# A gather-fed expert layer on one core: three of every four rows of the second table go to TensorE, one stays with VectorE

## The chip, the cores and the metric

The kernel runs on one core of a Trainium2 chip. The metric is the device time of one execution in microseconds (us); less is better. A core has TensorE (PE: matrix products, with its weight loads listed apart as PEld), VectorE (DVE), ScalarE (ACT), GpSimd (POOL) and SyncE (SP), each working through an instruction stream of its own in order and waiting for the others by semaphores, and sixteen DMA engines that they share.

## The reference

Two layers of a transformer-like block run over five blocks of 128 tokens (one of context, four latent). A layer is a mixer (four attention-like groups and an output product) followed by an expert layer. The mixer is unchanged here; the expert layer, cut to what matters, is this (`p` holds the layer's weights, `xb` is a block of 128 tokens by 1024):

```python
q = (xb @ p['peer_w_q']).reshape(128, 8, 2, 128)
s = jnp.einsum('thpd,pnd->thpn', q, p['peer_sub_keys'])
sv, si = lax.top_k(s, 16)
...
fv, fi = lax.top_k(cand, 16)
eid = jnp.take_along_axis(cid, fi, -1)      # 128 tokens x 8 heads x 16
gate = jax.nn.softmax(fv, -1)
act = jax.nn.gelu(einsum('thkd,td->thk', p['peer_u'][eid], xb))
out = einsum('thk,thkd->td', gate * act, p['peer_v'][eid])
```

So each token picks 8 x 16 rows of 1024 floats out of a first table (`peer_u`), takes a dot product with each, and sums as many rows of a second table (`peer_v`), each with a weight of its own. Everything is float32.

## The kernel before, in words

**Rows.** What is called a row here is one gather of 128 x 1024 floats (512 KB), one table row for each of the 128 tokens: 128 of `peer_u` and 128 of `peer_v` for each block of tokens, 2560 in the two layers. GpSimd issues each as an indirect DMA (L490) into one of the eight slots of `ring`. Before it fills a slot it waits until the row that lay there eight places earlier has been used (L486 to L489), and it does so in the order of the rows.

**Who uses a row.** A `u` row is always VectorE's: one multiply-and-sum with the token block gives a column of `dots` (L591). After the sixteen `u` rows of a head ScalarE takes the gelu (L526) and VectorE multiplies by the gates (L584), which gives `wsel`, the sixteen weights of the head. A `v` row is shared out by `on_pe` (L86): with `k` even it is TensorE's, with `k` odd VectorE's. VectorE adds its rows into `acc` with one instruction (L601). For TensorE, ScalarE first makes a 128 x 128 diagonal matrix out of one column of `wsel` (L533, four buffers in turn, `DIAGS`), and TensorE multiplies the row by it into `acc_ps`, two banks of PSUM (L559; the profile lists four matmuls for a row). The last sum of a token block adds `acc` and `acc_ps` (L425). Nothing of that depends on how many rows each of the two engines takes; `Experts.__init__` counts `by_pe` and `by_dve` along the order of the rows, and every wait is made from these counts.

**Order of rows.** `row_order` (L74) puts the rows of a step in one order for all engines. In a step with eight heads the first sixteen rows are `u`, then four `u` and four `v` in turn, and the last are `v`; in a step with fewer heads it is sixteen and sixteen.

**What the rows lie beside.** The expert layer of one token block runs while the mixer of another is worked on. Each step of the mixer gets an `Experts` object of one to eight heads (32 rows a head), and its code on each engine calls `rows(share)` at places written by hand: do all rows up to `share`/256 of the step's rows that are mine, then go on. TensorE, VectorE, ScalarE and GpSimd each have such calls, so that an expert row stands in the stream of its engine between two pieces of mixer work, and the mixer piece behind it waits for it. The steps that carry rows:

- `step_input` (L794): products with `w_in`, rotations, products for the latent queries; 71 to 90 us, one head. There are nine: four latent blocks in each of the two layers, and the second layer's context block. TensorE's calls are at L849 (`rows(16)`), L857 (between the products L855, `rows(16 + 32 * (i + 1))`), L893 (`rows(224)`) and L899 (`rows(256)`).
- `step_attend_route` (L1037): sixteen attention heads in some order, each of scores (L1140, L1141), a maximum on VectorE, an exponential on ScalarE (L1231), transposes (L1155, copied by ScalarE at L1238), products with the values (L1160) and a division on VectorE (L1325); then the output product `y` (L1172), the norm, the query product `w_q` in four chunks (L1192), and the routing, a long chain of searches on VectorE (top 16 of each half, then of the sums). It carries eight heads (six times), four (twice) or five (once, the context block). `SHARES` says how the rows are spread.
- `step_modulation(1)` (L668): the second layer's modulation, with two heads.
- `step_experts_only` (L1427): the last block's eight heads with no mixer work beside them.

Every step ends in a barrier of all engines (L365), which clears the semaphores. One more wait matters for the change: at L582 VectorE, before it overwrites one of the two halves of `wsel` with the weights of head `h`, waits until ScalarE has made all diagonals of head `h - 2`.

Of the kernel before, what the change touches and what calls it, by code (L numbers as in the profile page):

```python
# [33 lines left out]
PH, PK, TOPK = 8, 128, 16  # L34
# [22 lines left out]

RING = 8
HEAD_ROWS = 2 * TOPK
BY_PE = 2  # L60
DIAGS = 4
SHORT_TURN = 4

# [20 lines left out]


def on_pe(kind, k):  # L86
    return kind == "v" and k % BY_PE == 0


class Experts:  # L90
# [7 lines left out]
    def __init__(self, layer, block, first, heads, begin=False, end=False, ended=None):  # L98
        self.layer, self.block, self.first, self.heads = layer, block, first, heads
        self.begin, self.end, self.ended = begin, end, ended  # L100
        self.order = row_order(heads, SHORT_TURN if heads == PH else TOPK)

        self.by_dve, self.by_pe = [], []
        d = p = 0
        for kind, _, k in self.order:
            if on_pe(kind, k):
                p += 1
            else:
                d += 1
            self.by_dve.append(d)  # L110
            self.by_pe.append(p)

        self.before = block * PH + first + layer * (NBLK * PH)
# [10 lines left out]
def build(nc, a):  # L124
    es = ExitStack()
    with es:
# [5 lines left out]
        def sem(name):  # L132
            s = es.enter_context(nc.semaphore(name))
            sems.append(s)
            return s
# [216 lines left out]
        diag_done = sem("diag_done")  # L352
# [69 lines left out]
        def last_sum(dve, tiles):  # L422

            link = chain(dve, end_chain)
            link(dve.tensor_tensor(acc[:, :], acc[:, :], acc_ps, ALU.add))  # L425
            dve.wait_ge(end_in, 64)
            link(dve.tensor_tensor(acc[:, :], acc[:, :], tiles[1], ALU.mult))
            link(dve.scalar_tensor_tensor(acc[:, :], tiles[0], ALPHA, acc[:, :], ALU.mult, ALU.add))
            layer_norm(link, dve, acc[:, :], tiles[2], tiles[3], tiles[0], st12e, mve, vee[:, :], rstde[:, :],
                       end_var, end_rstd, 1).then_inc(end_done, 1)  # L430
# [38 lines left out]
        def experts_gpsimd(pool, E):  # L469
# [6 lines left out]
            def gather_until(n):  # L476
                while at[0] < min(n, len(E.order)):
                    r = at[0]
                    kind, h, k = E.order[r]
                    if kind == "u" and k == 0:  # L480
                        pool.tensor_copy(eid_s[:, h % 4, :], eid_e[:, ds((E.first + h) * TOPK, TOPK)]).then_inc(ids_staged, 1)  # L481
                        pool.wait_ge(ids_staged, h + 1)
                    if r >= RING:

                        q = E.order[r - RING]
                        if on_pe(q[0], q[2]):  # L486
                            pool.wait_ge(used_pe, E.by_pe[r - RING])
                        else:
                            pool.wait_ge(used_dve, E.by_dve[r - RING])  # L489
                    pool.indirect_dma_start(  # L490
                        ring[:, r % RING, :], None, a["peer_u"] if kind == "u" else a["peer_v"],
                        bass.IndirectOffsetOnAxis(ap=eid_s[:, h % 4, k:k + 1], axis=0)).then_inc(gath[r % RING], 16)
                    at[0] += 1
# [18 lines left out]
        def experts_scalar(act, E):  # L512
            if E is None:
                return lambda share: None
            at = [0, 0]

            def rows(share):
                while at[0] < E.target(share):
                    r = at[0]
                    kind, h, k = E.order[r]  # L520
                    if kind == "u" and k == TOPK - 1:

                        if h >= 2:
                            act.wait_ge(w_ready, h - 1)
                        act.wait_ge(used_dve, E.by_dve[r])
                        act.activation(gel[:, h % 2, :], dots[:, h % 2, :], ACT.Gelu_apprx_tanh).then_inc(gelu_sel, 1)  # L526
                    if on_pe(kind, k):
                        n = at[1]
                        if n >= DIAGS:
                            act.wait_ge(used_pe, n - DIAGS + 1)  # L530
                        act.wait_ge(w_ready, h + 1)

                        act.activation(diag[:, n % DIAGS, :], ident[:, :], ACT.Copy, scale=wsel[:, h % 2, k:k + 1]).then_inc(diag_done, 1)  # L533
                        at[1] += 1
                    at[0] += 1
            return rows
# [28 lines left out]
        def experts_vector(dve, E, in_psum=False):  # L565
            if E is None:
                return lambda share: None, lambda: None
            at = [0, E.begin]
            x2 = x2_ps if in_psum else x2e[:, :]

            def rows(share):
                while at[0] < E.target(share):
                    r = at[0]
                    kind, h, k = E.order[r]
                    if r == 0 and in_psum:
                        dve.wait_ge(x2_copied, 1)
                    if r == 0 and E.begin:
                        dve.wait_ge(e_in, 32)
                    if kind == "v" and k == 0:

                        if h >= 2:
                            dve.wait_ge(diag_done, (h - 1) * TOPK // BY_PE)  # L582
                        dve.wait_ge(gelu_sel, h + 1)
                        dve.tensor_tensor(wsel[:, h % 2, :], gel[:, h % 2, :], gates_e[:, ds((E.first + h) * TOPK, TOPK)], ALU.mult).then_inc(w_ready, 1)  # L584
                        dve.wait_ge(w_ready, h + 1)
                    if not on_pe(kind, k):
                        dve.wait_ge(gath[r % RING], E.landed(r))
                        if kind == "u":
                            if k == 0 and h >= 2:
                                dve.wait_ge(gelu_sel, h - 1)  # L590
                            dve.tensor_tensor_reduce(out=ring[:, r % RING, :], in0=ring[:, r % RING, :], in1=x2, scale=1.0, scalar=0.0,  # L591
                                                     op0=ALU.mult, op1=ALU.add, accum_out=dots[:, h % 2, k:k + 1]).then_inc(used_dve, 1)
                        else:
                            if at[1]:

                                dve.wait_ge(acc_zero, 2)
                                at[1] = False

                            if E.by_dve[r] > 1:
                                dve.wait_ge(used_dve, E.by_dve[r] - 1)  # L600
                            dve.scalar_tensor_tensor(acc[:, :], ring[:, r % RING, :], wsel[:, h % 2, k:k + 1], acc[:, :],  # L601
                                                     ALU.mult, ALU.add).then_inc(used_dve, 1)
                    at[0] += 1

            def finish():
                rows(256)
                if E.end:
                    dve.wait_ge(used_dve, E.by_dve[-1])
                    dve.wait_ge(used_pe, E.by_pe[-1])
                    last_sum(dve, [ring[:, i, :] for i in range(4)])  # L610

            return rows, finish


# [987 lines left out]
```

## Time and profile before

| | |
|---|---|
| median of three runs | 5474.67 us (5474.4 to 5474.68) |
| the profiled execution | 5474.31 us, its span 5472.5 us |
| PE busy | 3114.8 us (57%) |
| DVE busy | 3448.9 us (63%) |
| POOL busy | 2849.7 us (52%) |
| ACT busy | 629.9 us (12%) |
| mean granted TensorE clock | 0.759 |
| DMA, share of 16 engines | queue of POOL's gathers 67.1%, SP's queue 15.2% |

Busy time is the time in which an engine executes; the rest it waits or issues. No engine is busy for much more than half of the span, so the share of the whole says little, and the rows below are taken by stage. The granted clock is the share of full speed that TensorE was given (1.0 is 2.4 GHz, half of it 1.2 GHz).

### The profile page before, as it was taken

What the parts mean: (1) busy time and instruction counts of PE and PEld (TensorE: products, weight loads), DVE (VectorE), ACT (ScalarE), POOL (GpSimd) and SP (SyncE); (2) the same over time, 40 slices, a digit from 0 to 9 for tenths busy, and PEclk for the clock granted to TensorE, in tenths of its full rate; (3) what the DMA queues carried; (4) which work ended last, traced back from release to release, by engine and by line L of the source; (5) the groups of instructions that cost most, each with busy time, mean ns of one, the idle gap of its engine ahead of it and who ended that gap; (6) DMA issues with size and microseconds to landing.
All of it is one profiled execution on the core that took longest, in us unless ns stands there. A gap on an engine that the chain in (4) does not pass through costs nothing. (4 is left out here: it accounts for less than half of the span.)

```text
span 5472.5 us, 35115 instructions
## 1 busy us (share of the span) xinstructions
PE 3114.8 (57%) x9560; PEld 1611.1 (29%) x9560; DVE 3448.9 (63%) x6879; ACT 629.9 (12%) x1577; POOL 2849.7 (52%) x2830
## 2 busy tenths in 40 slices
PE   5647756357455645647545576655564564565354
PEld 1333334134123323411223233332232341233111
DVE  1255556666776856764468555567686677768765
ACT  0100121111011111000011001101101101111000
POOL 0015635366555645645446364445564665556675
PEclk9768858678677867878768787677786786777777
DMA  7537778789888988989888778768898898889998
GB/s 256 217 139 263 249 290 297 271 313 349 325 311 338 334 303 292 369 296 352 317 326 306 266 245 318 260 244 318 333 347 311 302 367 314 310 343 332 361 380 325
DMA packets 438293, 1667.46 MB, mean 305 GB/s; under 512 B 53072, under 2 KB 66448, under 8 KB 427504
## 3 DMA queue, kind: packets, MB, share of 16 engines
q0 software_dynamic: 369920, 1346.02, 67.1%
q1 hardware_dynamic: 68192, 319.31, 15.2%
q8 instruction: 78, 1.28, 0.1%
q14 instruction: 103, 0.84, 0.0%
HBM read 1637.48 MB, written 36.57 MB: 306 GB/s over the span
## 5 line engine op out<-in xcount | busy, mean ns | idle before, releaser
L559 PE MATMUL ps<-ring,diag 128*128 128x512 f32 x2560 | 1554.4, 757 | 1184.2 <-ACT diag L533 762.1
L490 POOL DMA_INDIRECT ring<-in_peer_v,eid_s x1280 | 1359.8, 1062 | 1080.0 <-PE ps L559 456.2
L490 POOL DMA_INDIRECT ring<-in_peer_u,eid_s x1280 | 1333.1, 1041 | 838.2 <-DVE dots L591 487.2
L591 DVE CUSTOM_DVE_ANT_0 ring<-ring,ps 128x1024 f32<-128x1024 f32 x1104 | 1305.7, 1217 | 124.2 <-DMA ring<-in_peer_u,eid_s 113.0
L559 PEld LDWEIGHTS ps<-ring,diag 128*128 128x128 f32 x2560 | 580.7, 241 | 2014.4 <-issue 1281.1
L601 DVE SCALAR_TENSOR_TENSOR acc<-ring,wsel,acc 128x1024 f32<-128x1024 f32 x640 | 827.4, 1293 | 484.5 <-DMA ring<-in_peer_v,eid_s 436.7
L855 PE MATMUL ps<-W,hT 128*128 128x512 f32 (+1 forms) x800 | 334.6, 581 | 60.6 <-DMA W<-in_w_in 44.2
L533 ACT ACTIVATE diag<-ident,wsel 128x128 f32<-128x128 f32 x640 | 225.4, 395 | 710.6 <-DVE wsel L584 393.8
L1192 PEld LDWEIGHTS ps<-hT,W 128*128 128x128 f32 x2560 | 294.5, 193 | 32.6 <-issue 17.7
L1192 PE MATMUL ps<-hT,W 128*128 128x128 f32 x2560 | 296.5, 277 | 11.6 <-ACT hT L1248 11.6
L591 DVE CUSTOM_DVE_ANT_0 ring<-ring,x2e 128x1024 f32<-128x1024 f32 x176 | 218.9, 1282 | 99.1 <-DMA ring<-in_peer_u,eid_s 98.8
L1140 PE MATMUL ps<-ktB,xs 64*128 64x512 f32 x64 | 49.3, 1130 | 310.1 <-DMA xs<-spill_state 174.0
L855 PEld LDWEIGHTS ps<-W,hT 128*128 128x128 f32 x800 | 158.0, 212 | 226.2 <-issue 181.9
L738 PE MATMUL ps<-W,condS 128*2 128x512 f32 x384 | 179.8, 628 | 26.8 <-DMA W<-in_b_ada 26.8
L1155 PE MATMUL ps<-ident,big 128*128 128x128 f32 x504 | 106.7, 352 | 134.6 <-ACT big L1231 134.5
L1299 DVE SCALAR_TENSOR_TENSOR big<-ps,toep 128x512 f32<-128x512 f32 x32 | 22.1, 689 | 253.7 <-DMA band<-in_c_band 211.2
L526 ACT ACTIVATE gel<-dots 128x16 f32<-128x16 f32 x80 | 17.2, 216 | 1384.0 <-DVE dots L591 1338.7
L481 POOL COPY eid_s<-eid_e 128x16 uint32<-128x16 uint32 (+1 forms) x80 | 17.2, 215 | 294.1 <-DMA eid_e<-expert_ids 214.5
L1325 DVE TENSOR_SCALAR aux<-ps,small 128x64 f32<-128x64 f32 x120 | 34.1, 284 | 191.8 <-PE ps L1160 189.8
L1172 PE MATMUL ps<-W,hT 128*128 128x512 f32 x320 | 141.6, 598 | 1.1 <-ACT hT L1243 1.1
L1155 PEld LDWEIGHTS ps<-ident,big 128*128 128x128 f32 x504 | 81.0, 183 | 184.3 <-ACT big L1231 143.4
L1238 ACT COPY big<-ps 128x512 f32<-128x512 f32 x96 | 56.2, 585 | 596.9 <-PE ps L1155 596.9
(203 smaller groups left out, 2849.1 us busy)
## 6 DMA issues: line engine op xcount, KB each, us to landing
W<-in_w_q SPq DMA_DIRECT2D x28, 2048.0 KB, 14.8
W<-in_w_ada SPq DMA_DIRECT2D x24, 2048.0 KB
W<-in_w_out SPq DMA_DIRECT2D x10, 4096.0 KB, 27.0
W<-in_w_in SPq DMA_DIRECT2D x16, 2048.0 KB, 16.2
ring<-in_peer_u,eid_s POOLq DMA_INDIRECT x1280, 6.4
ring<-in_peer_v,eid_s POOLq DMA_INDIRECT x1280, 6.1
xs<-x_state SPq DMA_DIRECT2D x20, 512.0 KB, 3.6
toep<-mod_rows SPq DMA_DIRECT2D x20, 512.0 KB, 7.9
```

Of the source, the lines that this page charges most:

```text
L490: pool.indirect_dma_start(ring[:, r % RING, :], None, a["peer_u"] if kind == "u" else a["peer_v"], bass.IndirectOffsetOnAxis(ap=eid_s[:, h ...
L533: act.activation(diag[:, n % DIAGS, :], ident[:, :], ACT.Copy, scale=wsel[:, h % 2, k:k + 1]).then_inc(diag_done, 1)
L559: last = pe.matmul(acc_ps[:, c * 512:(c + 1) * 512], diag[:, (E.by_pe[r] - 1) % DIAGS, :], ring[:, r % RING, c * 512:(c + 1) * 512], start ...
L591: dve.tensor_tensor_reduce(out=ring[:, r % RING, :], in0=ring[:, r % RING, :], in1=x2, scale=1.0, scalar=0.0, op0=ALU.mult, op1=ALU.add, a ...
L601: dve.scalar_tensor_tensor(acc[:, :], ring[:, r % RING, :], wsel[:, h % 2, k:k + 1], acc[:, :], ALU.mult, ALU.add).then_inc(used_dve, 1)
L738: last = pe.matmul(bank(c % NB, parts=2), condS[:, k, :], ada[:, c % NB, k, :], start=(k == 0), stop=(k == KD - 1))
L855: last = pe.matmul(bank(c, n), hT[:, k, :], w_in[c][:, k, :], start=(k == 0), stop=(k == KD - 1))
L1140: pe.matmul(near(i, lat), q, k[:, k0 * P:k0 * P + lat], start=True, stop=True)
L1155: last = pe.transpose(into, pr[:, i % 2, s * P:(s + 1) * P], ident[:, :])
L1172: last = pe.matmul(bank(2 + c), hT[:, k, :], w_out[:, k, c * 512:(c + 1) * 512], start=(k == 0), stop=(k == KD - 1))
L1192: last = pe.matmul(bank(2 + i % 2)[:, g * P:(g + 1) * P], w_q[c][:, k, g * P:(g + 1) * P], hT[:, k, :], start=(k == 0), stop=(k == KD - 1))
L1238: act.copy(prT[:, i % 2, 0:lat], near(i, lat))
```

## The change

Of the sixteen `v` rows of a head TensorE takes those with `k` mod 4 equal to 0, 1 or 2, which makes twelve, and VectorE those with `k` mod 4 equal to 3, which makes four; before it was eight and eight. The wait at L582 counts twelve diagonals a head in place of eight. All other counts follow from `on_pe`. The order of the rows, their places in the streams, the ring, the four diagonal buffers and the last sum are as before.

```diff
-BY_PE = 2
+PE_ROWS = TOPK * 3 // 4
 DIAGS = 4
...
 def on_pe(kind, k):
-    return kind == "v" and k % BY_PE == 0
+    return kind == "v" and k % 4 != 3
...
                         if h >= 2:
-                            dve.wait_ge(diag_done, (h - 1) * TOPK // BY_PE)
+                            dve.wait_ge(diag_done, (h - 1) * PE_ROWS)
```

## Rows read from the trace of the kernel before

**Rows 1.** The page: the span, and busy time of each engine with its share.

```profile
span 5472.5 us, 35115 instructions
PE 3114.8 (57%) x9560; PEld 1611.1 (29%) x9560; DVE 3448.9 (63%) x6879; ACT 629.9 (12%) x1577; POOL 2849.7 (52%) x2830
```

**Rows 2.** Groups of instructions, shapes apart: busy us, mean ns; then idle time before them.

```profile
L559 PE MATMUL ps<-ring,diag 128*128 128x512 f32 x2560 | 1554.4, 757 | 1184.2 <-ACT diag L533 762.1 <-DMA ring<-in_peer_v,eid_s 421.6
L490 POOL DMA_INDIRECT ring<-in_peer_v,eid_s x1280 | 1359.8, 1062 | 1080.0 <-PE ps L559 456.2 <-issue 270.9 <-DVE acc L601 179.9
L490 POOL DMA_INDIRECT ring<-in_peer_u,eid_s x1280 | 1333.1, 1041 | 838.2 <-DVE dots L591 487.2 <-issue 276.6 <-PE ps L559 41.7
...
L601 DVE SCALAR_TENSOR_TENSOR acc<-ring,wsel,acc 128x1024 f32<-128x1024 f32 x640 | 827.4, 1293 | 484.5 <-DMA ring<-in_peer_v,eid_s 436.7 <-PE ps L553 15.6 <-DVE big L1027 1.9
...
L533 ACT ACTIVATE diag<-ident,wsel 128x128 f32<-128x128 f32 x640 | 225.4, 395 | 710.6 <-DVE wsel L584 393.8 <-PE ps L559 316.6
```

**Rows 3.** Windows by stage: us; busy of PE, PEld, DVE, ACT, POOL; clock, DMA share, GB/s.

```profile
3211.00:3282.00 71.00, 55.56 (x157) 27.75 (x157) 40.79 (x75) 6.83 (x19) 46.07 (x46) 0.88 0.72 254
...
4165.00:4357.00 192.00, 103.54 (x312) 56.63 (x312) 136.48 (x247) 35.89 (x91) 110.78 (x110) 0.73 0.88 320
4357.00:4438.50 81.50, 47.15 (x121) 22.77 (x122) 51.64 (x79) 7.79 (x17) 44.67 (x46) 0.74 0.88 333
4438.50:4474.50 36.00, 36.00 (x234) 28.36 (x233) 24.49 (x32) 3.73 (x10) 26.93 (x27) 1.00 1.01 387
4484.00:4603.00 119.00, 61.76 (x96) 22.69 (x96) 111.50 (x280) 10.35 (x28) 78.86 (x69) 0.76 0.87 314
...
5076.30:5442.00 365.70, 180.09 (x260) 68.20 (x260) 247.88 (x339) 25.55 (x74) 266.63 (x265) 0.73 0.98 376
3353.00:3671.00 318.00, 188.61 (x692) 117.53 (x692) 207.18 (x480) 48.98 (x115) 131.85 (x134) 0.71 0.74 273
2412.00:2610.50 198.50, 129.36 (x271) 31.40 (x271) 78.01 (x112) 7.37 (x19) 83.68 (x67) 0.82 0.82 317
2701.00:3045.00 344.00, 161.04 (x556) 90.64 (x556) 230.56 (x503) 40.13 (x104) 169.30 (x168) 0.71 0.83 305
```

**Rows 4.** The same windows, line 559 alone: us; busy of PE and PEld (instructions); clock, DMA.

```profile
4165.00:4357.00 192.00, 57.58 (x88) 20.66 (x88) 0.73 0.88 320
4357.00:4438.50 81.50, 26.39 (x41) 9.81 (x42) 0.74 0.88 333
4438.50:4474.50 36.00, 14.26 (x32) 5.53 (x31) 1.00 1.01 387
4484.00:4603.00 119.00, 61.76 (x96) 22.69 (x96) 0.76 0.87 314
```

**Rows 5.** Timeline of one input step, 3211 to 3282: start, duration, instruction, [idle before].

```profile
3248.85 3.75 PE L559 MATMUL ps<-ring,diag 128*128 128x512 f32 x4 [4.99 <-ACT diag L533]
...
3260.12 3.60 PE L559 MATMUL ps<-ring,diag 128*128 128x512 f32 x8
...
3269.39 5.39 PE L559 MATMUL ps<-ring,diag 128*128 128x512 f32 x12 [1.13 <-ACT diag L533]
...
3276.28 3.67 PE L559 MATMUL ps<-ring,diag 128*128 128x512 f32 x8 [1.06 <-ACT diag L533]
...
3278.09 1.28 DVE L601 SCALAR_TENSOR_TENSOR acc<-ring,wsel,acc 128x1024 f32<-128x1024 f32 x1 [3.71 <-DMA ring<-in_peer_v,eid_s]
```

**Rows 6.** Waits over the whole span: total us, times, longest.

```profile
PE ps L1140 <- DVE aux L1325: 236.1, 80, 21.1
...
DVE aux L1325 <- PE ps L1160: 189.8, 64, 6.7
```

**Rows 7.** Timeline of the last step, which has expert rows alone.

```profile
5205.34 5.53 PE L559 MATMUL ps<-ring,diag 128*128 128x512 f32 x8 [5.16 <-ACT diag L533]
5206.08 1.28 DVE L601 SCALAR_TENSOR_TENSOR acc<-ring,wsel,acc 128x1024 f32<-128x1024 f32 x1 [1.38 <-DMA ring<-in_peer_v,eid_s]
5206.22 1.95 POOL L490 DMA_INDIRECT ring<-in_peer_u,eid_s  x1 [0.30 <-issue]
```

## The prediction

> **What bounds the kernel now.** I read the page's busy shares first [rows 1]: VectorE 63%, TensorE 57%, GpSimd 52%. None is near full, so no engine bounds the whole, and a mean over the span would mislead. The groups of instructions [rows 2] give the price of the two ways to use a row: four matmuls of 757 ns, 3.03 us when their overlapping records are added up, against one VectorE instruction of 1.293 us. Then I cut the span into stages [rows 3] and asked in each which engine is full. Four kinds show. In the stage of the query product (36 us) TensorE is busy 36.00 of 36 us. In the routing stage (119 us) VectorE is busy 111.50, 94%, TensorE 61.76. In the attention heads (192 us) neither is full: TensorE 103.54, VectorE 136.48; they hand work to and fro. In the last step, with expert rows alone, the DMA share is 0.98: the gathers set the pace. A fifth kind is the input step (71 us): TensorE 55.56, VectorE only 40.79. Last, the waits [rows 6] say who is late in the heads: TensorE waits for VectorE's L1325 236.1 us in 80 places, VectorE at L1325 for TensorE's L1160 189.8 us in 64.
>
> The difference between the two ways is thus not 3 us against 1.3; it depends on whose engine ends the stage. A row that TensorE gets behind other matmuls at full clock adds 1.79 us (12 matmuls take 5.39, 8 take 3.60 [rows 5]).
>
> **The change part by part.** Of 640 rows a side, 320 move: L559 goes from x2560 to x3840, L601 from x640 to x320. VectorE loses 320 x 1.293 = 414 us of work, TensorE gains as many rows, 320 x 1.79 = 573 us if all were at full clock, half of 1554.4 = 777 us by its present mean. What counts is which of it lies on a path.
>
> *Input steps, nine.* Of a head's 32 rows TensorE now has 1, 2, 3 and 2 in four blocks [rows 5]; by the new rule each block gets one more. The last block ends at 3279.95, VectorE's last row at 3279.37, and the step ends at 3282: TensorE ends last, and it stands in line from 3248.85 on, with idle gaps of about 1 us ahead of two blocks for a diagonal of ScalarE, which stay. Three rows are added at full clock, 5.4 us. The fourth joins a block that starts at half clock (one row took 3.75); two rows from a cold start took 5.53 elsewhere [rows 7], so it adds 1.8. Together 7.2; I take 7.0 a step, 63 us for nine. Bounds: 3.6 (only the last two blocks count, the front ones being lost in waiting) to 7.2, or 32 to 65. A gain has no way in here, since VectorE already ends first.
>
> *Eight-head steps, six.* The heads hold 88 matmuls of L559, 22 rows, at 57.58 / 22 = 2.62 us each [rows 4], and as many VectorE rows. Eleven move: +28.8 us on TensorE, -14.2 on VectorE. Neither engine is full, so each counts where it is the late one; by the waits [rows 6] that is TensorE in 189.8 / (189.8 + 236.1) = 0.45 and VectorE in 0.55 of the idle time. 0.45 x 28.8 - 0.55 x 14.2 = +5.2, bounds -14.2 to +28.8.
> In the output-product stage (81.5 us) about five rows move, at 2.57; two of them stand ahead of and between the products that VectorE waits for, 3.6, and I add 1 for the rest: +4.5, bounds -6.5 to +12.9.
> In the query stage TensorE is full and holds 8 rows in four chunks of two, 14.26 us, 1.78 each; each chunk gets a third: +7.2, bounds 0 to +7.2.
> In the routing stage 24 rows of each kind lie (x96 matmuls). Twelve VectorE rows leave, -15.5 at most; TensorE's 12 x 2.57 = 31 bring it from 62 to 93 of some 109 us, so it is still covered. The rows' transfers are the next bound: the share is 0.87 there and 0.98 at its highest in a long stretch, 119 x 0.87 / 0.98 = 105.6, so -13.4. I take -10, because TensorE's rows then release ring slots later; bounds -15.5 to 0.
> The gathers are shorter: where L601 runs, a gather takes 1.95 us [rows 7]; the means of 1041 and 1062 [rows 2] lie some 0.1 us above the undisturbed ones. Half of that, on the path in few places: -2 a step.
> Sum 5.2 + 4.5 + 7.2 - 10 - 2 = +4.9; six steps give 29.
>
> *Steps with four heads (two) and five (one).* With four heads 16 rows move. Query +7.2, output product +3.4, attention +2.6 (half of the above), routing -5: +8 a step, 16 in all. With five heads (TensorE 161.04 of 344 us, VectorE 230.56) 20 rows move, the same terms with a little less: +7. Bounds for the three, in sum: -20 to +70.
>
> *Modulation with two heads*: TensorE is busy 129.36 of 198.5 us, the DMA share 0.82; 8 rows move and cost at most 16. TensorE idles for a third of the stage, so I take a quarter: +4.
>
> *Expert rows alone.* VectorE 247.88 of 365.7 loses 32 x 1.293 = 41; TensorE goes from 180 to about 250 and stays covered. At 0.98 the transfers are full: -3, bounds -12 (the stretch of gathers goes) to +12 (a run of three TensorE rows releases its slots late).
>
> *Costed at nothing.* ScalarE makes 320 diagonals more at 0.395 = 126 us, on an engine that is busy for 12%; the cover is gone if a diagonal waits for its buffer (four of them; three TensorE rows in a run now need three) and ScalarE's next exponential is queued behind it. The wait at L582 asks for the diagonals of the head before the last, made long ago. Waits of the ring go on in the order of the rows; behind GpSimd's wait for a TensorE row stand all later gathers, so where TensorE comes late to a row, the following ones start late too, which the bounds of the heads hold.
>
> **Sum**: 63 + 29 + 16 + 7 + 4 - 3 = +116. The profiled execution took 5474.31, the median 5474.67, so the base is the same: 5590 us, 2.1% slower.
>
> **Weighed against the trace: the clock.** The granted clock is 0.71 to 0.76 in the heads and the routing, 1.00 where TensorE is full, 0.88 in the input step [rows 3]. A row costs 3.75 at 1.2 GHz alone and 1.79 more at 2.4 GHz. My sum leaves the clock of each stage as it is. The Trainium skill says in "TensorE: Matmul & The Clock Gate", Part 1, that the throttled state is the default and that activity releases it; by that, a TensorE with half again as many rows would run more of the time at full clock. By that the time is that of rival (a) below. The trace agrees in kind, with 1.00 in the stage that is full.
>
> **Rivals.** (a) *The clock rises* in the heads and with it everything of TensorE there. If the 33 rows a step then take 2.0 instead of 2.62, and the heads' other 46 us of matmul fall by a seventh, TensorE has 27 us less to do; at 0.45 on the path that is 12 a step, of which I let half come through beside VectorE's work, 6 x 6 = 36, and 9 in the three shorter steps: 45 less, 5545. For it: TensorE gets more work in just the stages at 0.73. Against it: a row still waits there for its gather and its diagonal, and the idle time stays. Chance 0.17.
> (b) *TensorE's rows stand in line in the heads, all of them*: each added row delays scores and products, and VectorE's relief only becomes waiting. Instead of +5.2, +28.8: 6 x 23.6 = 142, with 35 for the three shorter steps: 5767. For it: TensorE does its rows between two pieces of a head whether or not they are urgent. Against it: it idles almost half of the heads' time. Chance 0.15.
> (c) *The other side: VectorE is what ends each head*, so that the heads gain the 14.2 us of VectorE's rows. Place: L1325 and the maxima, of which TensorE waits 236.1 us. Price: -19.4 x 6 = -116 against my sum; with it the routing at its full -15.5 (-33 over six), half the heads' turn in the three shorter steps (-29) and -9 in the last step: 116 - 187 = -71, 5403. It decides from the point where the heads and routing together gain over 22 us a step of eight heads. For it: VectorE's 136 us against 104. Against it: the 64 places in which VectorE waits for TensorE. The gathers speak for it too, 1.95 us where a VectorE instruction with both operands in SBUF runs beside one. The Trainium skill, "SBUF — State Buffer", section "SBUF: two separate sides", calls the port pair of VectorE and GpSimd an exclusive lock, so that one of them blocks for the other's whole instruction; half of the rows of that kind gone would then free GpSimd. The trace shows the stretch of the gather and not that GpSimd is what most stages wait for. Chance 0.08.
> (d) *It comes out even*: the input steps hide their front blocks (32 instead of 63), the routing gains its most (-33) and the heads lean halfway to VectorE (-58): -6, about 5470. Chance 0.05.
> That the change doesn't do what it says can be left out: both engines follow one function.
>
> **Numbers.** Forecast 0.55, (a) 0.17, (b) 0.15, (c) 0.08, (d) 0.05. The range 5485 to 5720 holds the forecast with its bounds, (a) and half of (b); (c), (d) and the far part of (b) stay out. A difference of 0.2%, 11 us, is about what a measurement of this kernel can tell from no change. Slower: forecast, (a), (b) and a rest, 0.86; same 0.05; faster 0.09.
>
> **What would show it.** Right: input steps of 78 us in place of 71, chunks of the query stage 1.8 us longer, routing some 10 us shorter, the heads nearly unchanged, and VectorE's wait at L1325 for TensorE above 190 us while TensorE's for VectorE falls. The granted clock near 0.76 keeps (a) out; above 0.80 it is in. The heads at 220 us in place of 192 mean (b), at 178 (c). I am wrong if the input steps stay at 71 (TensorE was not their path), or if the last step moves by over 12 us.

## The result, and the profile after

The changed kernel takes 5634.28 us (median of four runs, 5622.78 to 5638.29) against 5474.53 before: a ratio of 1.0294, 95% interval 1.0276 to 1.0313, 160 us slower. The forecast was 5590, +116, with a range of 5485 to 5720. The direction and the mechanism of the largest term held. One term, the routing stage, failed, and in the middle of an eight-head step two stages exchanged a wait of 8 us that the forecast did not see and that costs nothing in sum. One execution, in the experiment on the middle of the eight-head step, ran at a granted clock of 0.558 and took 6995 us; the ratios leave it out.

The page of the changed kernel, its span and busy line, as in [rows 1]:

```profile
span 5636.3 us, 38001 instructions
PE 3591.1 (64%) x10840; PEld 1841.4 (33%) x10840; DVE 3042.6 (54%) x6559; ACT 742.2 (13%) x1897; POOL 2730.7 (48%) x2830
```

The groups that answer to [rows 2] (busy us, mean ns, then the idle time before them and its releasers):

```profile
L559 PE MATMUL ps<-ring,diag 128*128 128x512 f32 x3840 | 2047.4, 688 | 935.3 <-ACT diag L533 696.4 <-DMA ring<-in_peer_v,eid_s 238.6
...
L490 POOL DMA_INDIRECT ring<-in_peer_v,eid_s x1280 | 1305.5, 1020 | 1269.6 <-PE ps L559 838.5 <-issue 200.3 <-DVE dots L591 169.0
L490 POOL DMA_INDIRECT ring<-in_peer_u,eid_s x1280 | 1269.1, 991 | 878.6 <-DVE dots L591 494.2 <-issue 292.0 <-PE ps L559 69.9
...
L601 DVE SCALAR_TENSOR_TENSOR acc<-ring,wsel,acc 128x1024 f32<-128x1024 f32 x320 | 410.9, 1284 | 713.3 <-DMA ring<-in_peer_v,eid_s 686.5 <-issue 19.2 <-DVE big L1027 1.9
```

The counts are as foreseen, x3840 and x320. VectorE is 406 us less busy, TensorE 476 us more, and the span is 164 us longer. Two things catch the eye. A matmul of L559 became cheaper, 688 ns against 757, so a row costs 2.13 us in place of 2.43. And GpSimd, before it gathers a `v` row, now stands idle for TensorE 838.5 us where it was 456.2, although each gather is itself shorter (1020 and 991 ns against 1062 and 1041). The waits say the same; the first was 497.9 us before (456.2 and 41.7 in [rows 2]), the second 316.6:

```profile
POOL ring L490 <- PE ps L559: 908.4, 524, 11.3
...
ACT diag L533 <- PE ps L559: 632.9, 297, 9.9
...
DVE aux L1325 <- PE ps L1160: 323.2, 73, 8.7
...
PE ps L1140 <- DVE aux L1325: 208.8, 80, 21.5
```

In the heads the lateness has moved the way that was written down: VectorE's wait for TensorE at L1325 rose from 189.8 to 323.2 us, TensorE's for VectorE fell from 236.1 to 208.8 [rows 6].

**Where the time came from.** Both programs run the same mixer instructions in the same order, so the start of each step can be compared in the two traces and the difference split by steps. In the profiled executions (5636.3 - 5472.5 = +163.8), cut at the barrier L367 that ends each step:

| steps | foreseen | measured |
|---|---|---|
| nine input steps | +63 | +61 (5.2 to 8.3 each) |
| six eight-head steps | +29 | +74 (15.6, 16.3, 12.7, 9.9, 11.8, 7.7) |
| two four-head steps | +16 | +7 |
| the five-head step | +7 | +9 |
| modulation with two heads | +4 | +5 |
| expert rows alone | -3 | +9 |

The eight-head steps hold nearly the whole difference from the forecast, 45 of 48 us; the others come out even in sum. Split once more, by the first matmul of each stage, as a mean over the six steps:

| stage of an eight-head step | foreseen | measured |
|---|---|---|
| attention heads | +5.2 | +4.0 |
| output product | } +4.5 | +3.4 |
| norm and what follows, up to L1192 | } | -8.3 |
| query product | +7.2 | +14.8 |
| routing, to the next step | -10 | -1.3 |
| gathers, anywhere | -2 | not seen apart |

The windows of one such step show it. First the kernel before, cut at the first instructions of these stages (heads; output product and norm; query product; routing), columns as in [rows 3]:

```profile
4157.10:4364.70 207.60, 106.05 (x320) 57.84 (x321) 140.69 (x262) 37.39 (x93) 114.80 (x114) 0.71 0.89 325
4364.70:4434.70 70.00, 43.35 (x89) 18.97 (x89) 45.06 (x61) 5.60 (x13) 37.76 (x39) 0.75 0.86 327
4434.70:4477.30 42.60, 42.60 (x290) 34.95 (x291) 28.55 (x39) 4.43 (x12) 31.70 (x33) 1.00 1.01 383
4481.60:4606.70 125.10, 61.76 (x96) 22.69 (x96) 115.05 (x291) 10.35 (x28) 80.15 (x71) 0.76 0.85 307
```

and the changed kernel at the same instructions, with the input step that answers to 3211:3282 in [rows 3] and the last step behind them:

```profile
4292.50:4505.20 212.70, 122.33 (x364) 66.01 (x364) 127.62 (x251) 40.61 (x104) 107.86 (x114) 0.73 0.86 319
4505.20:4569.20 64.00, 47.92 (x108) 21.60 (x108) 34.72 (x49) 7.61 (x18) 35.53 (x37) 0.84 0.83 314
4569.20:4627.10 57.90, 52.23 (x306) 39.02 (x307) 29.62 (x45) 5.50 (x16) 32.37 (x35) 0.94 0.96 351
4631.40:4754.30 122.90, 79.50 (x144) 31.44 (x144) 99.94 (x279) 15.05 (x40) 70.56 (x69) 0.83 0.84 305
3318.80:3396.80 78.00, 62.87 (x173) 30.84 (x173) 35.22 (x71) 8.11 (x23) 45.74 (x47) 0.89 0.65 231
5231.60:5605.10 373.50, 221.64 (x388) 88.43 (x388) 206.56 (x307) 37.91 (x106) 256.00 (x265) 0.78 0.97 368
```

The routing line, 4631.40:4754.30, is the one to read slowly. VectorE does 99.94 us of work in place of 115.05, fifteen less, as foreseen, and the stage is 2 us shorter: VectorE now idles 23 of 123 us, TensorE is at 65% and GpSimd at 57%, no engine is full, and the DMA share did not rise (0.84 against 0.85). The clock rose there, 0.83 against 0.76, and in the output product, 0.84 against 0.75; in the heads it is 0.73 against 0.71.

The input step is plain. Its rows in the timeline of the changed kernel, as in [rows 5]:

```profile
3357.11 6.00 PE L559 MATMUL ps<-ring,diag 128*128 128x512 f32 x8 [4.99 <-ACT diag L533]
...
3370.25 5.31 PE L559 MATMUL ps<-ring,diag 128*128 128x512 f32 x12
...
3381.24 7.11 PE L559 MATMUL ps<-ring,diag 128*128 128x512 f32 x16 [1.13 <-ACT diag L533]
...
3389.85 5.39 PE L559 MATMUL ps<-ring,diag 128*128 128x512 f32 x12 [1.06 <-ACT diag L533]
3390.09 1.28 DVE L601 SCALAR_TENSOR_TENSOR acc<-ring,wsel,acc 128x1024 f32<-128x1024 f32 x1 [6.64 <-DMA ring<-in_peer_v,eid_s]
```

One row more in each block, 2.25 us in the first (6.00 against 3.75) and 1.72 in the others, 7.4 in all. TensorE's last row ends at 3395.24, VectorE's at 3391.37: the two ended within 0.6 us of each other before, and now TensorE is four late.

### The profile page after: what moved, and what is told of

Same layout as the page of the kernel before. It is cut to its first block and busy times, and to the rows that moved or that the text cites. A ratio compares the mean times of both kernels' runs of the same rounds, so it can differ in the third digit from the quotient of the medians.

```text
span 5636.3 us, 38001 instructions
## 1 busy us (share of the span) xinstructions
PE 3591.1 (64%) x10840; PEld 1841.4 (33%) x10840; DVE 3042.6 (54%) x6559; ACT 742.2 (13%) x1897; POOL 2730.7 (48%) x2830
## 5 line engine op out<-in xcount | busy, mean ns | idle before, releaser
L559 PE MATMUL ps<-ring,diag 128*128 128x512 f32 x3840 | 2047.4, 688 | 935.3 <-ACT diag L533 696.4
L490 POOL DMA_INDIRECT ring<-in_peer_v,eid_s x1280 | 1305.5, 1020 | 1269.6 <-PE ps L559 838.5
L490 POOL DMA_INDIRECT ring<-in_peer_u,eid_s x1280 | 1269.1, 991 | 878.6 <-DVE dots L591 494.2
L559 PEld LDWEIGHTS ps<-ring,diag 128*128 128x128 f32 x3840 | 821.6, 222 | 2040.5 <-issue 1548.1
L601 DVE SCALAR_TENSOR_TENSOR acc<-ring,wsel,acc 128x1024 f32<-128x1024 f32 x320 | 410.9, 1284 | 713.3 <-DMA ring<-in_peer_v,eid_s 686.5
L533 ACT ACTIVATE diag<-ident,wsel 128x128 f32<-128x128 f32 x960 | 338.2, 396 | 1017.8 <-PE ps L559 632.9
L1192 PEld LDWEIGHTS ps<-hT,W 128*128 128x128 f32 x2560 | 294.9, 193 | 32.0 <-issue 17.7
L1192 PE MATMUL ps<-hT,W 128*128 128x128 f32 x2560 | 296.9, 277 | 11.6 <-ACT hT L1248 11.6
L1325 DVE TENSOR_SCALAR aux<-ps,small 128x64 f32<-128x64 f32 x120 | 34.1, 284 | 324.9 <-PE ps L1160 323.2
```

Source lines behind the costliest of these rows:

```text
L490: pool.indirect_dma_start(ring[:, r % RING, :], None, a["peer_u"] if kind == "u" else a["peer_v"], bass.IndirectOffsetOnAxis(ap=eid_s[:, h ...
L559: last = pe.matmul(acc_ps[:, c * 512:(c + 1) * 512], diag[:, (E.by_pe[r] - 1) % DIAGS, :], ring[:, r % RING, c * 512:(c + 1) * 512], start ...
L1192: last = pe.matmul(bank(2 + i % 2)[:, g * P:(g + 1) * P], w_q[c][:, k, g * P:(g + 1) * P], hT[:, k, :], start=(k == 0), stop=(k == KD - 1))
```

## The experiments

All experiments are built on one edit of the changed kernel that, read in the code, changes no instruction by itself: which rows are TensorE's is kept as a list by row of the step, and all counts, the wait at L582 too, are made from it. `MOST` is three rows in four, `HALF` the two of the kernel before, `FEW` one. Each experiment then changes one line, shown below; where the division isn't that line, it is `MOST`.

```diff
-def on_pe(kind, k):
-    return kind == "v" and k % 4 != 3
+MOST, HALF, FEW = (0, 1, 2), (0, 2), (0,)
+def on_pe(heads, r, h, k):
+    return k % 4 in MOST
...
-                            dve.wait_ge(diag_done, (h - 1) * PE_ROWS)
+                            dve.wait_ge(diag_done, sum(p for p, o in zip(E.pe, E.order) if o[1] < h - 1))
```

The kernel before varied between 5459 and 5483 us over these comparisons, so the ratios with their intervals are read, and a difference in us is the ratio applied to the median beside it.

### The input steps alone

```diff
+    return k % 4 in (MOST if heads == 1 else HALF)
```

> The new division (three rows in four to TensorE) in the nine input steps with one head alone; everywhere else eight and eight as before. Theory A, TensorE ends these steps: each gets some 7 us longer, +62 us in all, about 5537 us, and no other step moves. Rival, what the changed kernel showed there was passed on from the steps before: under +30 us. Seen in the trace as the last L559 of the step ending about 7 us later in the input step, VectorE's last L601 not.

Ratio 1.0112 (1.0092 to 1.0132), +61 us. The end of the same input step as above in this kernel's timeline:

```profile
3319.07 5.39 PE L559 MATMUL ps<-ring,diag 128*128 128x512 f32 x12 [1.06 <-ACT diag L533]
3319.18 1.28 DVE L601 SCALAR_TENSOR_TENSOR acc<-ring,wsel,acc 128x1024 f32<-128x1024 f32 x1 [6.51 <-DMA ring<-in_peer_v,eid_s]
```

TensorE ends at 3324.46, VectorE at 3320.46, and the steps of other kinds keep their length within 3.5 us each. The largest term of the forecast stands by itself.

### The eight-head steps alone

```diff
+    return k % 4 in (MOST if heads == PH else HALF)
```

> The new division in the steps with eight heads alone (six of the mixer and the last one with expert rows alone); input steps, modulation and the steps with four and five heads as before. Theory A, the parts add up: six steps of about +12 us and +8 us in the last one, +83 us, about 5557 us. Rival, the eight-head steps lose because the steps before them leave rows or a clock that is different: less than half of it, under +40 us.

Ratio 1.0119 (1.0097 to 1.0141), +65 us; 53 to 77 by the interval, a little under the 83 expected and clear of the rival's 40. The stages of the steps move as in the changed kernel (output product +2.7 to +4.2, norm, here only up to the transposes L1180, -6.5 to -7.9, query +12.4 to +16.0). Input and eight-head steps together make 126 of the 160 us; the table has 22 for the four- and five-head steps and the modulation, and the intervals, 11 to 12 us to either side, leave room for the other 12.

### An even tail

```diff
+    return k % 4 in (HALF if heads == PH and h == PH - 1 else MOST)
```

> The changed kernel, but the last head of every eight-head step is divided eight and eight again; its sixteen v rows are the last rows of the step, done in one run while the routing ends. Theory A, the routing stage gave VectorE's saving back because TensorE does twelve of these sixteen rows in line after VectorE is through: four rows of 1.8 us less, -5 to -7 us a step, -30 to -45 us for the six and the last step, about 5595 us. Rival B, the gathers behind the ring set the pace of the last rows whoever takes them: within 10 us of the changed kernel, about 5634 us.

Ratio 1.0295 (1.0276 to 1.0314), the same as the changed kernel: theory A falls. The number is rival B's, but the gathers are not the whole reason. In the changed kernel VectorE's routing chain (its last product, L1421) ends 109.2 us after the stage begins, as a mean over the six steps, 4.8 earlier than before (113.9), yet the stage ends at 122.9 against 124.2, with TensorE's last row at 121.3. I had taken these last TensorE rows for the price. With the tail even TensorE has less to do, but the four rows go back into VectorE's stream ahead of and between its last products: its chain ends at 113.4 and the stage at 124.1. The window of this stage in one step, to be held against 4631.40:4754.30 above:

```profile
4628.80:4752.50 123.70, 73.94 (x128) 28.86 (x128) 105.05 (x283) 13.63 (x36) 71.57 (x69) 0.82 0.84 303
```

TensorE has 5.6 us less to do there, VectorE 5.1 more, and the length is the same. What one engine saves the other pays.

### Eight diagonals in place of four

```diff
-DIAGS = 4
+DIAGS = 8
```

> The changed kernel with eight buffers for the diagonal matrices in place of four, so that ScalarE waits less for TensorE before it makes one. Theory A, TensorE's own time for the rows is the price: no more than 10 us less than the changed kernel, 5625 to 5640 us. Rival C, ScalarE stands at a diagonal (its waits for TensorE at L533 rose from 317 to 633 us) and holds up copies and exponentials behind it: 40 us or more come back, under 5595 us.

Ratio 1.0303 (1.0281 to 1.0325), no different from 1.0294. The waits of this kernel:

```profile
POOL ring L490 <- PE ps L559: 896.0, 506, 11.4
...
DVE aux L1325 <- PE ps L1160: 320.5, 74, 9.4
...
ACT diag L533 <- PE ps L559: 196.7, 97, 8.5
```

ScalarE's wait for TensorE fell from 633 to 197 us, and neither GpSimd's wait, nor VectorE's, nor the time moved. The doubled wait at L533 in the profile of the changed kernel was a wait that nobody paid for; the cover named in the prediction for the diagonals held.

### The input steps the other way

```diff
+    return k % 4 in (FEW if heads == 1 else HALF)
```

> The other way in the nine input steps alone: TensorE takes one row in four, VectorE three; everywhere else eight and eight as before. Theory A, TensorE ends these steps: four rows of 1.8 us less, less what VectorE now adds at the end, -3 to -6 us a step, -27 to -54 us, about 5432 us. Rival, VectorE's four rows more end the step: within 10 us of before, about 5471 us.

Ratio 1.0002 (0.9991 to 1.0014): nothing, the rival's case. The end of the input step:

```profile
3255.64 9.63 DVE L601 SCALAR_TENSOR_TENSOR acc<-ring,wsel,acc 128x1024 f32<-128x1024 f32 x7 [0.21 <-DVE big L1027]
...
3259.56 1.96 PE L559 MATMUL ps<-ring,diag 128*128 128x512 f32 x4 [1.06 <-ACT diag L533]
...
3266.07 1.28 DVE L601 SCALAR_TENSOR_TENSOR acc<-ring,wsel,acc 128x1024 f32<-128x1024 f32 x1 [0.80 <-DMA ring<-in_peer_v,eid_s]
```

TensorE is done at 3261.52, almost 6 us ahead, and VectorE, with seven rows in a run, ends the step at 3267.35. The next step starts at the same time as before. Eight and eight is a balance in these steps: a row more on TensorE costs 1.7 us, a row less earns nothing.

### Half the work of a row, in the routing

```diff
-                        for c in range(2):
+                        for c in range(1 if E.heads == PH and r >= 180 else 2):
```

> The changed kernel, but in the eight-head steps TensorE multiplies only the first 512 of the 1024 columns of each row from the 180th of the step on (the routing stage, its tail, and the last part of the step with expert rows alone); the other half of these products is left out. Counts, waits, order and the ring are the same; a row costs TensorE half. Theory P, TensorE's runs of three rows hold the ring slots and the tail: the routing stage gets 6 to 10 us shorter in six steps, -36 to -60 us, about 5585 us. Theory V, the stage goes by VectorE's searches, the dots queued behind them and the weights that wait for the dots: under -15 us, above 5620 us.

Ratio 1.0215 (1.0181 to 1.0250), 43 us under the changed kernel (52 by the medians), inside theory P's range. The window of the same routing stage:

```profile
4592.70:4710.10 117.40, 57.25 (x72) 18.87 (x72) 99.82 (x279) 15.06 (x40) 70.85 (x69) 0.67 0.86 318
```

TensorE is busy 57 us in place of 79.5, for 36 rows of two matmuls each; the clock fell to 0.67. As a mean over the six steps the stage takes 116.7 us in place of 122.9, and VectorE's chain ends at 104.0 in place of 109.2. Against the kernel before that is -7.4, near the -10 that was foreseen. VectorE's searches are not shortened by this edit and the rows it has are the same, so it is TensorE's time for its rows that kept this part of the saving away. Where it went in VectorE, the waits of the stage show, in the kernel before, the changed kernel and this one:

```profile
POOL ring L490 <- PE ps L559: 12.3, 6, 6.3
...
DVE acc L601 <- DMA ring<-in_peer_v,eid_s: 5.5, 4, 2.2
```

```profile
POOL ring L490 <- PE ps L559: 23.6, 16, 8.2
...
DVE acc L601 <- DMA ring<-in_peer_v,eid_s: 16.5, 6, 5.1
```

```profile
POOL ring L490 <- PE ps L559: 13.6, 13, 6.8
...
DVE acc L601 <- DMA ring<-in_peer_v,eid_s: 12.9, 5, 4.4
```

GpSimd waits for TensorE before it may gather, and VectorE waits for the gathers of its own `v` rows. For `u` rows VectorE waits under 1 us here in any of the three. In the last step, too, the rows end after 365.5 us in place of 372.4 (before: 364.1).

### Three in four in the routing alone

```diff
+    return k % 4 in (MOST if heads == PH and r >= 180 else HALF)
```

> Three rows in four to TensorE only from the 180th row of an eight-head step on (routing stage, tail, and the last part of the step with expert rows alone); everything else eight and eight. Theory A, the routing stage alone gains what the changed kernel showed there, about -2.5 us in six steps and no loss elsewhere: -5 to -20 us, about 5459 us. Rival, the gain of the stage is paid for by later gathers in the next step or in the last step: 0 to +10 us.

Ratio 1.0016 (1.0007 to 1.0026), +9 us: the rival's side. The routing stage is 1.0 us shorter than before as a mean, the last step 2.3 longer, and the rest, 0.9 in the heads and 0.7 in the norm as means, I cannot assign. This division gets nothing out of the stage where VectorE is busiest.

### The mirror: one in four everywhere

```diff
+    return k % 4 in FEW
```

> The mirror of the change: TensorE takes one row in four everywhere, VectorE three. Theory A, the stages count: nine input steps of -3 to -6 us, output product and query stage of the eight-head steps -3, heads -4 to +7 and routing +10 to +15 by VectorE's twelve rows more; in sum -40 + 6 x 10 = +20 us, 5450 to 5540 us. Rival, TensorE's time is the price throughout and the mirror gains what the change lost: below 5400 us.

Ratio 1.0134 (1.0110 to 1.0158), +73 us, more than theory A's +20 and far from the rival. The routing stage takes 135.5 us as a mean, +11.4, as foreseen. The query stage takes 6.9 us more, but the norm ahead of it 5.7 and the output product 3.1 less, so that the middle gains 1.9 a step where 3 was expected. In the profiled executions (+75) the six eight-head steps make +72 and the last step +9. The input steps gain nothing, as in the experiment on them above; theory A had counted on -40 there.

### The middle of the eight-head step even

```diff
+    return k % 4 in (HALF if heads == PH and 108 <= r < 180 else MOST)
```

> The changed kernel, but rows 108 to 180 of every eight-head step (they lie beside the output product, the norm and the query product) are divided eight and eight again. Theory A, the stages of the trace add up: output product +3.4, the norm behind it -7.7, query stage +14.8 all go, -10.5 in six steps and a little in the last step: -55 to -70 us, about 5572 us. Rival, these figures were passed on from the rows of the heads before: less than half of it, above 5605 us.

Ratio 1.0170 (1.0139 to 1.0202), against 1.0294: -68 us. Output product, norm (up to L1180) and query stage are back to within 1 us of the kernel before in all six steps. The three figures of the table belong to these 72 rows and to each other.

### The query rows even

```diff
+    return k % 4 in (HALF if heads == PH and 148 <= r < 180 else MOST)
```

> The changed kernel, but only rows 148 to 180 of every eight-head step (beside the query product) are divided eight and eight again. Theory A, of the query stage's +14.8 the four rows more in its chunks make 7 and the late weights at its entry the rest, which the rows before it cause: -5 to -8 us in six steps, -30 to -48 us, about 5595 us. Rival, the rows of the stage make all of it: -75 us or more, below 5560 us.

Ratio 1.0226 (1.0204 to 1.0247): -37 us, 6.2 a step, theory A. The query window with the whole middle even, and with the query rows alone even:

```profile
4519.30:4561.90 42.60, 42.59 (x290) 34.94 (x291) 30.20 (x42) 4.43 (x12) 32.78 (x34) 1.00 1.03 408
```

```profile
4539.30:4590.80 51.50, 44.69 (x290) 35.71 (x291) 33.38 (x46) 4.43 (x12) 33.10 (x33) 0.93 0.98 374
```

In the second TensorE has the same 290 matmuls and idles 6.8 us: it waits at the entry for a diagonal. In this kernel the norm is 8.3 us shorter than before and the query stage 8.3 longer, as means; the 14.8 of the changed kernel are these 8.3 and 6.5 for the four rows. What the diagonal waits for, the timelines show. First the changed kernel:

```profile
4554.23 1.58 SPq L1092 DMA_DIRECT2D W<-in_w_q  x2
...
4556.91 0.97 POOL L490 DMA_INDIRECT ring<-in_peer_u,eid_s  x1 [0.49 <-POOL eid_s L481]
...
4560.31 6.87 PE L559 MATMUL ps<-ring,diag 128*128 128x512 f32 x12 [10.82 <-ACT diag L533]
...
4564.01 0.94 POOL L490 DMA_INDIRECT ring<-in_peer_v,eid_s  x1 [2.40 <-PE ps L559]
...
4572.70 1.22 DVE L591 CUSTOM_DVE_ANT_0 ring<-ring,ps 128x1024 f32<-128x1024 f32 x1 [4.51 <-DMA ring<-in_peer_u,eid_s]
...
4577.90 0.17 DVE L584 TENSOR_TENSOR wsel<-gel,gates_e 128x16 f32<-128x16 f32 x1
...
4578.71 7.90 PE L559 MATMUL ps<-ring,diag 128*128 128x512 f32 x12 [5.67 <-ACT diag L533]
```

and the kernel before at the same place:

```profile
4411.81 1.25 SPq L1092 DMA_DIRECT2D W<-in_w_q  x2
...
4412.86 1.94 POOL L490 DMA_INDIRECT ring<-in_peer_v,eid_s  x1 [6.23 <-DVE acc L601]
...
4415.11 0.95 POOL L490 DMA_INDIRECT ring<-in_peer_v,eid_s  x1 [0.30 <-issue]
...
4417.79 0.97 POOL L490 DMA_INDIRECT ring<-in_peer_u,eid_s  x1 [0.28 <-POOL eid_s L481]
...
4428.04 3.78 PE L559 MATMUL ps<-ring,diag 128*128 128x512 f32 x4 [5.00 <-DMA ring<-in_peer_v,eid_s]
...
4434.69 3.84 PE L1192 MATMUL ps<-hT,W 128*128 128x128 f32 x32 [1.16 <-ACT hT L1248]
...
4435.66 0.17 DVE L584 TENSOR_TENSOR wsel<-gel,gates_e 128x16 f32<-128x16 f32 x1
```

When the norm is through, SyncE loads two pieces of `w_q`, 2 MB each (L1092). In the changed kernel the first `u` row of the next head is gathered 2.7 us after that (4556.91), ahead of TensorE's run of three (4560.31) and of GpSimd's wait for it (4564.01), so the run does not hold it up. It lands late: the four `u` rows take 15.8 to 16.2 us from issue to landing, where the median of all gathers is 6.2, and the DMA share from 4554 to 4572.5 is 1.01. VectorE waits 4.51 us for the first of them, the weights of the next head come at 4577.90, and TensorE, with half a chunk of the query product done, waits 5.67 us for a diagonal; its next three rows take 7.90 us at a mean granted clock of 0.68.

Before, the `u` rows were gathered 6.0 us after the load and took 12.9 us, and the weights came no later: 23.8 to 25.0 us after the load over the six steps, against 23.5 to 25.0 in the changed kernel. What moved is the query product. Before, GpSimd stood 6.23 us behind a row that VectorE does only after the norm; TensorE's last row ahead of the transposes was gathered after the load (4415.11), TensorE waited for it, and the query product began 21.5 to 23.3 us after the load. Now TensorE's three rows are gathered before the load, the product begins 14.9 to 15.7 us after it, and it meets the wait for weights that come no earlier. So the norm lost a wait and the query product got it, and in sum it costs nothing. That the load is what holds the gathers up is read from the trace; no run moves it.

### The same number, in pairs

```diff
+    return k % 4 in (0, 1)
```

> Eight and eight as before, but TensorE takes k mod 4 equal to 0 and 1, VectorE 2 and 3, so that each has two rows in a run where they took turns. Theory R, a run of TensorE rows holds ring slots and so the gathers behind it, apart from what the rows cost by their number: +10 to +40 us, about 5495 us. Rival, the number alone counts: within 10 us of before, about 5472 us.

Ratio 1.0085 (1.0060 to 1.0111), +47 us, with no engine doing more work (TensorE 3111.9 us busy, VectorE 3443.4). The order in which two engines share the rows costs over a quarter of what the change cost. In the profiled executions (+39) the six eight-head steps make +32, the nine input steps +24 and the last step +4. In the eight-head steps the middle shows the same exchange as in the changed kernel (norm -7.5, query +8.2 as means), and the routing takes 3.7 us more; VectorE's wait for its `v` rows there rises by 3.4. But the expectation named TensorE's runs, and in the input steps it is VectorE's: its last row now ends 2 to 5 us later than before and 2 to 3 after TensorE's. And the two four-head steps are 9.0 and 10.4 us shorter (317.5 to 308.4, 317.6 to 307.2), where in runs that leave their division alone they move by at most 3.4. So a run does not cost everywhere; why these steps gain is open, and no run has pairs in them alone.

### The heads alone

```diff
+    return k % 4 in (MOST if heads == PH and r < 108 else HALF)
```

> Three rows in four to TensorE only in the first 108 rows of an eight-head step (beside the sixteen attention heads, and the first part of the last step); everything else eight and eight. Theory A, the heads cost what the changed kernel showed there, +4 in six steps, and the last step +3: +15 to +40 us, about 5498 us. Rival, VectorE's relief counts in the heads by itself and the loss came from other rows: 0 or less, 5472 us or below.

Ratio 1.0058 (1.0035 to 1.0082), +32 us (19 to 45). The 108 rows lie beside twelve heads of nine rows each (`NH` is 12, and L1325 has 120 instructions in ten steps), not sixteen. The heads take +3.0 as a mean (-0.3 to +8.6), and the stages behind them move by less than 1.5 us. VectorE's relief of 14 us a step is worth nothing there.

## Why the prediction was right and where it was wrong

**Input steps**: +63 foreseen, +61 measured and +61 alone. The path was read rightly from the two ends, 0.6 us apart. What was not said, and the other direction showed, is that this path is no wider than those 0.6 us: it was right to price a row more on TensorE at its full 1.8, and it would have been wrong to price a row handed to VectorE as a gain.

**Heads**: +5.2 foreseen, +4.0 measured, +3.0 alone. Dividing the idle time by who waits for whom gave the right size of the mean; the six steps spread from -0.1 to +10.1, so one such agreement may be luck. Rivals (b), all in line, and (c), VectorE ends each head, are both out: the heads of the step shown went from 207.6 to 212.7 us, where (b) asked for 28 more and (c) for 14 less.

**Output product and query stage**: +4.5 and +7.2 foreseen, 11.7 together; measured +3.4 - 8.3 + 14.8 = +9.9. Of the query stage's +14.8 the four rows in the chunks are 6.2 to 6.5, near the sum's 7.2; the other 8.3 are the wait that the norm lost. So both terms were about right, 3.4 for 4.5 and 6.5 for 7.2, and the exchange, which the prediction did not see, adds nothing.

**Routing**: this step failed, in size. VectorE's rows were to save 15.5 us, the transfers to leave 13.4 of it, and the late release of ring slots by TensorE's rows to take 3.4 more: -10, and -2 for shorter gathers. TensorE's 31 us more were "still covered", since 93 of some 109 us leave room. Measured: -1.3, inside the bounds. VectorE does work 15.1 us less, but it idles 13.8 us more. As means over the six steps it waits 16.8 us for the gathers of its own `v` rows where it was 4.8 (for `u` rows 0.5 where it was 0.3), and GpSimd waits 23.2 us for TensorE's rows where it was 12.7. So the term that was mis-sized is, in good part at least, the late release, given 3.4 us. TensorE has room in the mean, but a row is not covered by TensorE's idle time elsewhere: it is used in the order of the ring, and each row of VectorE is now gathered behind three of TensorE's. With half the price of TensorE's rows GpSimd's wait is back at 13.1, and 6.2 of the missing 10.7 us come back; the diagonals brought none, a different division of the tail none. What the other 4.5 us are I have not settled: even then VectorE waits 13.1 us for its rows. No run has a ring with more slots. Six times this error is 64 us; the heads and the middle give back 18, which leaves 46, and the eight-head steps exceed their term by 45.

**Expert rows alone**: -3 foreseen, +9 measured, inside the bounds of -12 to +12 and by the mechanism that stood at their upper end, a run of three rows that releases its slots late: GpSimd's waits for TensorE in this step rose from 6.7 to 35.6 us, and with half the price of the later rows 6.9 us come back.

**The clock**: rival (a) is half there. The mean granted clock is 0.788 against 0.759, between the two marks that were set (0.76 and 0.80), a row costs 2.13 us in place of 2.43, and TensorE's rows take 493 us more in place of the 573 to 777 foreseen. The Trainium skill says in "TensorE: Matmul & The Clock Gate", Part 1, that activity releases the throttle. The trace agrees in the output product (0.84 against 0.75) and the routing (0.83 against 0.76); in the heads, where the rival put the gain, it is only 0.73 against 0.71. What the rise gave back no run shows by itself; the time came out above the forecast all the same.

**The gathers** are shorter, GpSimd is 119 us less busy, and nothing of it can be seen in the time: GpSimd's waits for TensorE rose from 497.9 to 908.4 us in its place. The Trainium skill, "SBUF — State Buffer", section "SBUF: two separate sides", calls the port pair that VectorE and GpSimd share an exclusive lock. The trace agrees in the durations: a gather that takes 0.94 us elsewhere took 1.95 beside L601 [rows 7], and with half of L601's rows gone the means fell. So this argument for rival (c) holds, and rival (c) falls even so.

No version beat the kernel before: three in four costs 160 us, one in four 73, the same number in pairs 47, and three in four in the one stage that looked made for it 9. One in four in the input steps alone is even with it.

## What to carry to other kernels

When two engines take turns at buffers that are refilled in order, the idle time of an engine need not cover a longer run of its items: ask who waits for the slots, and whose item is fetched behind them. Before pricing a shift of work from one engine to the other, read the ends of both in each stage: where they lay within a microsecond here, the loss was the full price and the gain in the other direction zero. When a stage grows by a new wait, look whether the stage ahead of it lost one, and when the transfer behind the wait was issued. And a wait that doubles in the profile is no cost until taking it away moves the time.

## What was not expected

That the order alone, with equal work on every engine, costs 0.85% in sum, and that two of the steps gain by it. That ScalarE's wait of 633 us at the diagonals could be cut to 197 without any effect. And that the same matmul got 9% cheaper in the mean (757 to 688 ns) in a kernel that got slower.
